# Two weight buffers, a mixed block order and a delayed down projection in a mixture-of-experts stage

## The reference, cut to what matters

```python
for e in range(MOE_EXPERTS):                       # 32 experts
    hid = jax.nn.silu(h @ w1[e]) * (h @ w3[e])     # 1024 -> 512, twice
    out = out + gates[:, e:e + 1] * (hid @ w2[e])  # 512 -> 1024
```

## Time and profile before

| | |
|---|---|
| median of 3 runs | 1173.06 us |
| the profiled execution | 1177.17 us, its span 1174.5 us |
| PE busy | 937.2 us (80%) |
| DVE, ACT, POOL busy | 425.7, 244.9, 150.1 us |
| weight queue (SP) | 246.04 MB, 55.4% of 16 DMA engines' span |
| gather and scatter queue (POOL) | 18.27 MB, 6.3% |

### The profile page before, as it was taken

The page is one execution under the profiler, slowest core; times in us unless marked ns, Lnnn a source line. Parts: engine busy times, 40 slices in busy tenths (PEclk is TensorE's granted clock), DMA queues, the critical chain, the costliest instruction groups (busy, mean ns, idle before and its releaser), DMA issues.

```text
span 1174.5 us, 11671 instructions
## 1 busy us (share of the span) xinstructions
PE 937.2 (80%) x3833; PEld 445.2 (38%) x3833; DVE 425.7 (36%) x1078; ACT 244.9 (21%) x527; POOL 150.1 (13%) x385
## 2 busy tenths in 40 slices
PE   4789999885899988996699995777777777777770
PEld 1355554663444444446344442222222222222220
DVE  3347556744768664136211111122112111211115
ACT  4411002204445454112011010011101110110103
POOL 4110100210000000000001112121212121211202
PEclk9899999868899998995699998999999999999995
DMA  9941210512071940004178985999999999999965
GB/s 309 359 126 62 37 72 0 112 18 90 1 287 63 212 121 1 18 36 162 25 299 298 341 310 183 412 406 400 389 387 369 394 357 399 371 399 366 345 260 219
DMA packets 60912, 264.78 MB, mean 225 GB/s; under 512 B 11208, under 2 KB 13568, under 8 KB 41936
## 3 DMA queue, kind: packets, MB, share of 16 engines
q1 hardware_dynamic: 48256, 246.04, 55.4%
q0 software_dynamic: 12448, 18.27, 6.3%
q10 hardware_dynamic: 176, 0.05, 0.0%
HBM read 266.18 MB, written 22.26 MB: 246 GB/s over the span
## 4 chain that ended last, share of the span: by engine, by line
issue 42%; PE 37%; DVE 7%; DMA 5%; POOL 4%; ACT 3%; POOLq 1%; SPq 0%; DVEq 0%; ACTq 0%
PE PS L691 10%; PE PS L924 5%; PE PS L826 3%; DMA W<-in_w_mod 3%; POOL held L539 2%; PE PS L995 2%; PE PS L601 2%; PE PS L650 2%; PE PS L849 2%; PE PS L837 1%; DVE sml L1700 1%; PE PS L854 1%; ACT MP L1199 1%; PE PS L759 1%; PE PS L935 1%
## 5 line engine op out<-in xcount | busy, mean ns | idle before, releaser
L992 PE MATMUL PS<-W,S5R 128*64 128x512 f32 x800 | 190.2, 620 | 57.4 <-DMA W<-in_moe_w 57.3
L691 PE MATMUL PS<-W,HTR 128*128 128x512 f32 (+2 forms) x352 | 144.0, 568 | 3.2 <-DVE MP L1427 3.2
L1012 PE MATMUL PS<-W,S5R 128*64 128x512 f32 x400 | 95.3, 620 | 51.1 <-ACT S5R L1278 31.7
L992 PEld LDWEIGHTS PS<-W,S5R 128*64 128x64 f32 x800 | 56.0, 142 | 189.1 <-DMA W<-in_moe_w 94.5
L1271 ACT ACTIVATE S5R<-PS 128x256 f32<-128x256 f32 (+1 forms) x31 | 13.2, 425 | 435.2 <-PE PS L992 352.6
L691 PEld LDWEIGHTS PS<-W,HTR 128*128 128x128 f32 x352 | 66.7, 198 | 71.5 <-issue 67.8
L1957 DVE TENSOR_TENSOR S5R<-S5R,PS 128x256 f32<-128x256 f32 x25 | 10.5, 421 | 219.5 <-ACT S5R L1271 219.5
L995 PE MATMUL PS<-W,S5R 128*128 128x512 f32 x192 | 86.9, 611 | 2.5 <-ACT S5R L1263 2.4
L1969 DVE TENSOR_TENSOR S5R<-PS,QKV 64x512 f32<-64x512 f32 x50 | 34.4, 688 | 124.2 <-PE PS L1012 123.4
L539 POOL TENSOR_TENSOR held<-held 1x1 f32<-1x1 f32 x147 | 26.9, 183 | 402.1 <-PE PS L977 171.9
L1012 PEld LDWEIGHTS PS<-W,S5R 128*64 128x64 f32 x400 | 28.4, 142 | 101.9 <-issue 101.9
(11 more groups left out here) (409 smaller groups left out, 1080.6 us busy)
## 6 DMA issues: line engine op xcount, KB each, us to landing
W<-in_moe_w SPq DMA_DIRECT2D x124, 1024.0 KB, 9.1
W<-in_moe_w SPq DMA_DIRECT2D x31, 2048.0 KB, 11.5
W<-in_w_mod SPq DMA_DIRECT2D x12, 2048.0 KB, 8.6
W<-in_w_in SPq DMA_DIRECT2D x3, 2048.0 KB, 13.3
QKV<-in_x SPq DMA_DIRECT2D x8, 512.0 KB, 14.7
W<-in_w_out SPq DMA_DIRECT2D x2, 2048.0 KB, 15.3
S5R<-k_d POOLq DMA_DIRECT2D x16, 128.0 KB, 6.1
xh_d<-S5R POOLq DMA_DIRECT2D x4, 512.0 KB, 3.0
```

Of the source, the lines that this page charges most:

```text
L691: ins = mm(dst[:, c0:width], hT[:, k, tok], wslot(n, width)[:, k, c0:width], start=(k == 0), stop=(k == KD - 1))
L992: ins = mm(PS[r, 1024:1536].rearrange("p (m h) -> p m h", m=2), hgT[:, k, 0:64], w13[:, :, k, 256 * m:256 * m + 256], start=(k == 0), stop ...
L1012: ins = mm(PS[64 * n:64 * n + 64, 2560:3072], hidT[:, k % 2, 64 * (k // 2):64 * (k // 2) + 64], w2s[:, k, 512 * n:512 * (n + 1)], start=(k ...
```

## The change

1. **Two buffers.** `W`, `HTR` and `MP` become parts of one tensor `BIG`, and of it two sets of w1, w3 and w2 are cut (`w13(side)`, `w2s(side)`). Blocks use them in turn. A load of block b now waits for the use of block b-2, and for the landing of block b-1's load of the same kind.
2. **Block order.** Positions 0, 3, 6, ... up to a last one are full, two half blocks lie between each pair of them, and the remaining half blocks follow. TensorE, ScalarE and VectorE run six steps per loop iteration for it. The number of full positions is made odd: 7 here (positions 0, 3, ..., 18), of which the last holds a half block that runs as a full one. `nblk` stays 31. The table and `slots` are computed through a map `virt` from position to the old order.
3. **Step order.** In every step the order is `up(b), turn_rows(b+1), down(b-1), turn_hid(b)`, for half blocks too.

GpSimd's loop of gathers and scatters is unchanged.

```diff
-NBLK = NE + (LAT * TOPK - NE) // P
+NSIX = (LAT * TOPK // 65 + 1) // 2
+NBLK = 6 * NSIX + 7
...
-        w13 = W[:, 0:2, :].rearrange("p m (k h) -> p m k h", k=KD)
-        w2s = W[:, 2, :].rearrange("p (k d) -> p k d", k=4)
+        XB = BIG[:, 0:8 * 3072].rearrange("p (s m n) -> p s m n", s=2, m=3)
+        def w13(side):
+            return XB[:, bass.ds(side, 1), 0:2].rearrange("p s m (k h) -> p (s m) k h", k=KD)
+        def w2s(side):
+            return XB[:, bass.ds(side, 1), 2].rearrange("p s (k d) -> p (s k) d", k=4)
...
             def next13(b):
                 e = expert(b)
                 for piece in range(2):
-                    sp.wait_ge(sem("w13_used"), 2 * b + piece - 1)
+                    if piece == 0:
+                        sp.wait_ge(sem("w13_in0"), 32 * b)
+                    if not isinstance(b, int) or b >= 2:
+                        sp.wait_ge(sem("w13_used"), 2 * b + piece - 3)
+                    if piece == 1:
+                        sp.wait_ge(sem("w13_in1"), 32 * b)
                     for m in range(2):
-                        load13(e, m, piece)
-            def next2(b):
-                e = expert(b)
-                sp.wait_ge(sem("w2_used"), b)
-                load2(e)
+                        load13(e, b, m, piece)
+            def before2(after):
+                e = expert(after - 1)
+                if not isinstance(after, int) or after >= 3:
+                    sp.wait_ge(sem("w2_used"), after - 2)
+                sp.wait_ge(sem("w2_in"), 16 * after - 16)
+                load2(e, after - 1)
             next13(1)
-            with sp.Fori(2, nful + 1) as b:
-                next13(b)
-                next2(b - 1)
-            next2(nful)
-            with sp.Fori(nful + 1, nblk) as b:
-                next13(b)
-                next2(b)
+            next13(2)
+            before2(2)
+            with sp.Fori(3, nblk) as b:
+                next13(b)
+                before2(b)
+            before2(nblk)
...
+            def step(b, half, half_before, side):
+                up(b, half, side)
+                turn_rows(b + 1)
+                down(b - 1, half_before, 1 - side)
+                turn_hid(b, half)
             turn_rows(0)
-            up(0, False)
+            up(0, False, 0)
             turn_rows(1)
             turn_hid(0, False)
-            with pe.Fori(1, nful) as b:
-                up(b, False)
-                turn_rows(b + 1)
-                down(b - 1, False)
-                turn_hid(b, False)
-            up(nful, True)
-            turn_rows(nful + 1)
-            down(nful - 1, False)
-            turn_hid(nful, True)
-            down(nful, True)
-            with pe.Fori(nful + 1, nblk - 1) as b:
-                up(b, True)
-                turn_rows(b + 1)
-                turn_hid(b, True)
-                down(b, True)
-            up(nblk - 1, True)
+            with pe.Fori(1, tail, 6) as b:
+                for i in range(6):
+                    step(b + i, i % 3 < 2, i % 3 > 0, 1 - i % 2)
+            step(tail, True, False, 1)
+            step(tail + 1, True, True, 0)
+            with pe.Fori(tail + 2, nblk - 2, 2) as b:
+                step(b, True, True, 1)
+                step(b + 1, True, True, 0)
+            step(nblk - 2, True, True, 1)
+            up(nblk - 1, True, 0)
+            down(nblk - 2, True, 1)
             turn_hid(nblk - 1, True)
-            down(nblk - 1, True)
+            down(nblk - 1, True, 0)
...
+            st(stt(virt, is_half, nf1, back, ALU.mult, ALU.subtract))
+            st(ts(below, io_f[:, :], low_end, None, ALU.is_lt))
+            st.settle()
+            st(tt(virt, virt, below, ALU.mult))
+            st.settle()
+            st(tt(virt, virt, io_f[:, :], ALU.add))
+            st.settle()
```

More of the change, by code:

```diff
@@ L140, in build @@
         slots = sb("slots", [P, NBLK, 2], I32)
+        io_i, tok_i = slots[:, :, 0], slots[:, 0:NLT, 1]
         btab = sb("btab", [1, NBLK + 2], I32)
@@ L225, in build @@
         cum = rt[:, 1640:1736].rearrange("p (t e) -> p t e", t=NLT - 1)
+        virt, is_half, back, below = (rt[:, 1800 + 64 * i:1800 + 64 * i + NBLK] for i in range(4))
+        nf1, low_end = rt[:, 2060:2061], rt[:, 2061:2062]
         wexp, nful = rt[:, 1568:1569], rt[:, 1569:1570]
@@ L351, in _, with load13 @@
             sp.dma_start(fng, a["final_norm_g"].partition_broadcast(P)).then_inc(sem("fng_in"), 16)
-            def load13(e, m, piece):
+            def load13(e, b, m, piece):
                 src = a["moe_w1" if m == 0 else "moe_w3"][0]
@@ L357, in load13, with load2 @@
                 src = src.rearrange("e (p k) n -> p (e k) n", k=KD)[:, KH * piece:KH * (piece + 1), :]
-                sp.dma_start(w13[:, m, KH * piece:KH * (piece + 1), :], src).then_inc(sem(f"w13_in{piece}"), 16)
-            def load2(e):
+                sp.dma_start(w13(b % 2)[:, m, KH * piece:KH * (piece + 1), :], src).then_inc(sem(f"w13_in{piece}"), 16)
+            def load2(e, b):
                 src = a["moe_w2"][0]
                 src = src[e:e + 1] if isinstance(e, int) else src[bass.ds(e, 1)]
-                sp.dma_start(w2s, src.rearrange("e (k p) n -> p (e k) n", p=P)).then_inc(sem("w2_in"), 16)
+                sp.dma_start(w2s(b % 2), src.rearrange("e (k p) n -> p (e k) n", p=P)).then_inc(sem("w2_in"), 16)
             slot_free = [NL - 1 - (NL - 1 - m) % RING for m in range(RING)]
             sp.wait_ge(*used(slot_free[1]))
-            load13(0, 1, 0)
-            load13(0, 1, 1)
+            load13(0, 0, 1, 0)
+            load13(0, 0, 1, 1)
             sp.wait_ge(*used(slot_free[0]))
-            load13(0, 0, 0)
-            load13(0, 0, 1)
+            load13(0, 0, 0, 0)
+            load13(0, 0, 0, 1)
             sp.wait_ge(*used(slot_free[2]))
-            load2(0)
+            load2(0, 0)
             sp.wait_ge(sem("routed"), 1)
-            nful = sp.value_load(btab[0:1, NBLK:NBLK + 1], min_val=0, max_val=NBLK - 5) + 2
-            nblk = sp.value_load(btab[0:1, NBLK + 1:NBLK + 2], min_val=0, max_val=NBLK - 5) + 5
+            nblk = 2 * sp.value_load(btab[0:1, NBLK + 1:NBLK + 2], min_val=0, max_val=(NBLK - 13) // 2) + 13
             def expert(b):
@@ L529, in _ @@
             pool.wait_ge(sem("hg_clear"), 1)
-            nblk = pool.value_load(btab[0:1, NBLK + 1:NBLK + 2], min_val=0, max_val=NBLK - 5) + 5
+            nblk = 2 * pool.value_load(btab[0:1, NBLK + 1:NBLK + 2], min_val=0, max_val=(NBLK - 13) // 2) + 13
             cells = {}
@@ L947, in _ @@
             ends = PS[0:NE, 2562:2564]
+            mm(PS[:, 2564:2565], ones[0:NE, :], fhv[0:NE, 0:1], start=True, stop=True)
             mm(ends, tri_inc[0:NE, :], fhv[0:NE, :], start=True, stop=False)
@@ L967, in _ @@
             pe.wait_ge(sem("routed"), 1)
-            nful = pe.value_load(btab[0:1, NBLK:NBLK + 1], min_val=0, max_val=NBLK - 5) + 2
-            nblk = pe.value_load(btab[0:1, NBLK + 1:NBLK + 2], min_val=0, max_val=NBLK - 5) + 5
+            tail = 6 * pe.value_load(btab[0:1, NBLK:NBLK + 1], min_val=0, max_val=NSIX - 1) + 7
+            nblk = 2 * pe.value_load(btab[0:1, NBLK + 1:NBLK + 2], min_val=0, max_val=(NBLK - 13) // 2) + 13
             def turn_rows(b):
@@ L978, in turn_rows, with up @@
                 ins.then_inc(sem("hg_tr"), 1)
-            def up(b, half):
+            def up(b, half, side):
                 pe.wait_ge(sem("hgT_a"), b + 1)
@@ L992, in up @@
                                 ins = mm(PS[r, 1024:1536].rearrange("p (m h) -> p m h", m=2), hgT[:, k, 0:64],
-                                         w13[:, :, k, 256 * m:256 * m + 256], start=(k == 0), stop=(k == KD - 1))
+                                         w13(side)[:, :, k, 256 * m:256 * m + 256], start=(k == 0), stop=(k == KD - 1))
                             else:
-                                ins = mm(bank(2 + m), hgT[:, k, :], w13[:, m, k, :], start=(k == 0), stop=(k == KD - 1))
+                                ins = mm(bank(2 + m), hgT[:, k, :], w13(side)[:, m, k, :], start=(k == 0), stop=(k == KD - 1))
                     ins.then_inc(sem("w13_used"), 1)
@@ L1002, in turn_hid, with down @@
                 ins.then_inc(sem("hid_t"), 1)
-            def down(b, half):
+            def down(b, half, side):
                 pe.wait_ge(sem("hidT"), b + 1)
@@ L1012, in down @@
                             ins = mm(PS[64 * n:64 * n + 64, 2560:3072], hidT[:, k % 2, 64 * (k // 2):64 * (k // 2) + 64],
-                                     w2s[:, k, 512 * n:512 * (n + 1)], start=(k == 0), stop=(k == 3))
+                                     w2s(side)[:, k, 512 * n:512 * (n + 1)], start=(k == 0), stop=(k == 3))
                 else:
@@ L1256, in _ @@
             act.wait_ge(sem("perm_in"), 16)
-            nful = act.value_load(btab[0:1, NBLK:NBLK + 1], min_val=0, max_val=NBLK - 5) + 2
-            nblk = act.value_load(btab[0:1, NBLK + 1:NBLK + 2], min_val=0, max_val=NBLK - 5) + 5
```

(36 more changed lines are left out.)

44 lines of the change are left out of this document (27 added, 17 removed).

## The result

The changed kernel takes 1238.3 us (median of 4 runs, 1233.4 to 1243.4) against 1170.8 for the kernel before in the same set: ratio 1.056, 95% interval [1.051, 1.061]. It is slower, as forecast, but by 67.5 us instead of 24, and lies just above the stated range (1235). The profiled execution has a span of 1239.2 us, 64.7 more than before.

What follows compares the result with a forecast made beforehand. Full blocks bound by PE, half blocks by loading; after the change, the gather loop. 615 + 552 = 1167 for the last down, against 1142.8 before: +24 on the median of 1173.1, 1197 us; range 1162 to 1235.

Steps and rivals of the forecast that it cites:

- The mechanism: Half steps: closed loop of down, results, scatter, gather, transpose; transposes start 12.3 us after the last down, PE idles 4.8.
- the signs named: Experts' stage: weight waits nearly gone, 80 to 120 us of gather waits, DMA share near 0.9, half periods of 18 us.
- The sum: Positions 1 to 28 and the last two downs: 552 us after down(0) ends at 615, so last down ends at 1167.
- The landing g: Gather's time from issue to landing, counted 22 times: 7.8 us, with 6.3 and 10.0 as bounds.
- The slow stretch behind a wait: Downs after a gather wait run partly at the lower clock: 7.69 us full, 3.65 + 0.66 = 4.3 half.
- the 10.0 of the earlier trace: One earlier gather's landing in us, with a scatter 2.1 us ahead and a block's loads just issued.
- a stretch with 1.7 us of extra time: A half block's piece of up: 5.35 us after an idle of 2.92, against 3.65 after one of 1.88.
- rival 1: Gathers in the experts' stage land in 6.3 us as DMA engines partly idle: 1164 us; chance 0.12 faster, 0.10 same.
- Rival 2: Experts' stage: the gather loop does not bind and loading does, 29 blocks of 16.4 us: 1101 us; chance 0.06.
- Rival 3: Gathers land in 10.0 us, since scatter and gather always follow within 2.1 us: +48 us, 1245; chance 0.10.
- Rival 4: PE's six-step loop: two jumps back each stall for code loading, 0 to 10 us in all: 1202 us; chance 0.05.

Runs made afterwards that it cites:

- e1: The changed kernel with only GpSimd's order edited: gather(b+3) goes ahead of scatter(b), once block b+2's rows are transposed; 1131.3 us, ratio 0.965 to the kernel before.
- e9: The changed kernel with gather(b+3) still waiting for results(b) but issued ahead of scatter(b); 1168.5 us, ratio 0.995 to the kernel before.

## Why the prediction was right in kind and wrong in size

**The mechanism was right, point by point.** Weights are no longer waited for; half steps wait for the gather, 22 times, behind down, results and scatter; full steps cover it; down(0) was forecast to end at 615 and ended at 616.1; what follows the last down is 31.6 us against 31.7. e1 opens the loop and e9 shortens it, and the time follows both. The 616.1 is in part luck: gather(0) was issued 2.3 us later than before, not 1, and landed in 9.0 us, not 7.8, while up(0) took 15.64 us instead of the 17.02 put. Of the signs named, the size of three was missed with the time: waits of 130.9 us (80 to 120 forecast), a DMA share of 0.83 between 590 and 1180 us (0.9), half periods of 20.5 us late in the stage (18).

**The sum was 40.6 us short.** The last down ends at 1203.95 + 3.65 = 1207.6, not 1167. Of that, 1.1 us are the start. Two terms of the sum were mis-sized and have most of the rest, about 22 and 15 us:

- *The landing g, 7.8 us.* The 22 gathers that PE waited for took 8.8 us in the mean, which is 22 us too little in the sum. (PE's idle time was forecast at 22 x 4.8 = 106 us and is 130.9.) They are of two kinds. Six go out behind the scatter of a real full block (positions 0, 3, ..., 15): 9.1 to 11.1 us, 9.9 in the mean. The other 16 take 8.4 in the mean, that behind position 18, a half block run as full, among them with 8.0. The median of the earlier trace rows came from gathers that had no scatter 2.1 us ahead of them. In e9, where the scatter goes out behind, the same places have 8.5 and 7.7: so the scatter ahead is worth about 1.4 and 0.7 us. A full block's scatter alone does not make 10: the gathers of the earlier trace rows also had one 2.1 us ahead and took 5.6 to 6.8, with the DMA engines at 0.87. The prediction had the 10.0 of the earlier trace rows before it and gave it to a rival for all 22 instead of to these six. Why these six are still slower than the others in e9 was not tested.
- *The slow stretch behind a wait, 0.66 us per down.* Half downs were forecast at 16 x 4.3 + 8 x 3.65 = 98 us and took 111.7; the seven full ones 53 and took 54.7. That is the 15 us. The 0.66 came from one wait of 2.46 us. Measured behind the waits, it is 1.5 us in the mean for the 16 half downs (4.3 to 5.7 us each) and 0.9 for the six full ones. It does not grow with the wait that precedes it, as these two show:

```profile
630.03 1.97 PE L992 MATMUL PS<-CST,S5R 128*128 128x128 f32 x8 [6.68 <-DMA S5R<-xh_d,gidx]
631.93 4.28 PE L1027 MATMUL PS<-BIG,S5R 128*64 128x512 f32 x16
...
1043.58 1.97 PE L992 MATMUL PS<-CST,S5R 128*128 128x128 f32 x8 [5.35 <-DMA S5R<-xh_d,gidx]
1045.48 5.71 PE L1027 MATMUL PS<-BIG,S5R 128*64 128x512 f32 x16
```

In e9, with waits of 2.0 to 4.9 us, it is still 1.2 us for a half down. What sets its size stays open. The earlier trace rows held a stretch with 1.7 us of extra time, which the prediction cited and did not use for its sum.

**The rivals.** Faster gathers (rival 1) did not come where they count: the DMA share of the stage fell to 0.80 to 0.87, but, as argued, not during the gather's flight (second row; the first is the stretch before it):

```profile
1023.40:1035.30 11.90, 11.90 (x46) 4.75 (x48) 2.74 (x6) 1.89 (x5) 1.69 (x5) 0.76 0.63 241
1035.35:1043.58 8.23, 2.88 (x15) 0.73 (x11) 0.42 (x1) 0.38 (x1) 1.54 (x4) 0.95 1.03 422
```

The six gathers behind which a full up runs did land in 4.1 to 5.6 us, but nothing waited for them. Rival 2 is what e1 makes of the kernel, so its rule (loading binds once the gather is out of the way) was right, its condition not met; its 1101 us was 30 us below e1's 1131.3, some 12 of them since blocks took 16.83 us. Rival 3's 10 us held for the gathers behind a full block's scatter only. Rival 4, code loading: between PE's steps at position 6 to 7, the jump back to the six-step loop's head, nothing stands still (nor at the other, at 842.6 us):

```profile
716.05 0.66 PE L1016 MATMUL PS<-CST,S5R 128*128 128x128 f32 x4
716.64 7.09 PE L1007 MATMUL PS<-BIG,S5R 128*64 128x512 f32 x32
```

The Trainium skill's rule on taken branches (Runtime: NRT & Kernel Launch, Instruction fetch mechanics) therefore costs nothing that shows here. The Trainium skill's rule that DMA engines take packets in turn from their queues (DMA: Bandwidth & Descriptors, Queues, rings and completion order) fits e1, where more loads are in flight (a 2 MB load lands in 16.7 us instead of 8.8) and gathers still take 8.1 to 8.2 us.

**The range** ended at 1235 because the slow-gather rival was cut off at the top. Both mis-sized terms point the same way, and the slope of 22 waits per us of g was known: the upper bound ought to have been that rival's full size.

## What to carry to other kernels

When work is delayed behind the next block's, follow every queue that the delayed work feeds: here one scatter kept its place ahead of a gather that had nothing to do with it, and two good changes looked like a loss of 5.6% where moving the gather ahead of it gives a gain of 3.5%. A closed loop through engines and a DMA has a period of its own, and it must be compared with both the busiest engine and the loads before a gain is counted from either. Price a DMA's landing by rows with the same neighbours in flight, and price an idle gap on TensorE as the gap plus the slower work behind it.

## What was not expected of the hardware

- Adding 105 us of filler products to TensorE made the kernel 40 us faster in span and 34.5 in the medians (e2): the granted clock of the execution was 0.937 instead of 0.882.
- Halving the bytes of loads that nobody waited for made it 71 us faster in span (e3): the landing of a gather fell from 8.2 to 5.8 us and that of a scatter from 7.2 to 3.6.
